# VectorE makes the lower parts of five weight units in the first FFN chunk, and the input forms are made in another order

## What is computed

```
def swiglu_ffn(h, w_gu, w_down):            # w_gu 1024 x 5632, w_down 2816 x 1024
    gate, up = jnp.split(h @ w_gu, 2, axis=-1)
    return (jax.nn.silu(gate) * up) @ w_down

for layer in range(2):
    x = x + mixer(rms_norm(x, mix_norm[layer]))
    x = x + swiglu_ffn(rms_norm(x, ffn_norm[layer]), w_gu[layer], w_down[layer])
```

## Time and profile before

| | before |
|---|---|
| median of 3 runs | 2703.15 us (2702.84 to 2703.3) |
| the profiled execution's own time | 2702.78 us |
| its span | 2701.0 us |
| TensorE busy in the span | 99% |
| VectorE, ScalarE, GpSimd busy | 47%, 31%, 47% |
| granted TensorE clock, mean | 0.998 |

### The profile page before, as it was taken

One profiled execution on the slowest core, in us unless ns is written; L12 is line 12 of the kernel. 1 busy time (PEld: TensorE's weight loads), 2 busy tenths in 40 slices (PEclk: granted clock), 3 DMA queues, 4 the chain that ended last, 5 costly groups with the idle time before them and its releaser, 6 DMA issues.

```text
span 2701.0 us, 35201 instructions
## 1 busy us (share of the span) xinstructions
PE 2672.0 (99%) x12017; PEld 2213.0 (82%) x12017; DVE 1273.9 (47%) x1719; ACT 831.3 (31%) x1388; POOL 1267.7 (47%) x1208
## 2 busy tenths in 40 slices
PE   8999999999999999999999999999999999999998
PEld 6888888888888788888888788888887888888887
DVE  8333322323334854444444447365688444444444
ACT  4120120120124533333333515234365222222224
POOL 4324323323423455655555454363454556655555
PEclk9999999999999999999999999999999999999999
DMA  4101102111111111111121021111111111111212
GB/s 143 44 28 63 44 28 63 47 32 59 48 36 44 51 51 54 47 47 54 53 64 51 27 60 44 36 55 40 44 55 47 55 54 47 47 47 55 69 50 83
DMA packets 173768, 139.29 MB, mean 52 GB/s; under 512 B 9200, under 2 KB 143472, under 8 KB 173680
## 3 DMA queue, kind: packets, MB, share of 16 engines
q1 hardware_dynamic: 171584, 133.46, 16.2%
q10 hardware_dynamic: 2096, 4.62, 0.5%
HBM read 132.81 MB, written 5.24 MB: 51 GB/s over the span
## 4 chain that ended last, share of the span: by engine, by line
PE 95%; DVE 3%; ACT 1%; issue 1%; DMA 0%; SPq 0%; DVEq 0%
PE ps L773 31%; PE ps L777 31%; PE ps L776 31%; DVE f_h_lo L2144 1%; PE ps L1085 0%; PE ps L1009 0%; PE ps L849 0%; PE ps L911 0%; DMA residual<-in_x 0%; DVE gate_buf L2082 0%; DVE f_h_lo L2133 0%; DVE h_sum_a L2133 0%; DVE gate_buf L2222 0%; ACT f_h_hi L1581 0%; DVE h_sum_a L2158 0%
## 5 line engine op out<-in xcount | busy, mean ns | idle before, releaser
L602 POOL TENSOR_TENSOR f_w_lo<-f_raw,f_w_hi 128x512 fp32r<-128x512 f32 x270 | 357.5, 1326 | 449.6 <-ACT f_w_hi L1532 364.6
L773 PE MATMUL ps<-f_h_hi,f_w_hi 128*128 128x512 f32 x1232 | 481.1, 390 | 3.6 <-DVE f_h_lo L2144 2.3
L777 PE MATMUL ps<-f_h_hi,f_w_lo 128*128 128x512 f32 x1232 | 479.5, 389 | 0.0
L776 PE MATMUL ps<-f_h_lo,f_w_hi 128*128 128x512 f32 x1232 | 479.4, 389 | 0.0
L560 POOL TENSOR_TENSOR small<-w_raw 128x1 f32<-128x1 f32 x200 | 59.5, 297 | 804.6 <-PE ps L773 794.1
L2333 DVE TENSOR_TENSOR residual<-ps,residual 128x512 f32<-128x512 f32 x352 | 239.4, 691 | 170.5 <-PE ps L777 170.4
L773 PEld LDWEIGHTS ps<-f_h_hi,f_w_hi 128*128 128x128 f32 x1232 | 231.2, 188 | 57.2 <-issue 4.4
L1532 ACT ACTIVATE f_w_hi<-f_raw 128x512 fp32r<-128x512 f32 x246 | 155.1, 631 | 382.9 <-PE ps L777 382.8
L777 PEld LDWEIGHTS ps<-f_h_hi,f_w_lo 128*128 128x128 f32 x1232 | 231.3, 188 | 48.3
L776 PEld LDWEIGHTS ps<-f_h_lo,f_w_hi 128*128 128x128 f32 x1232 | 231.3, 188 | 47.2
L773 PE MATMUL ps<-f_w_hi,f_act_hi 128*128 128x512 f32 x688 | 267.8, 389 | 0.0
(11 more groups left out here) (305 smaller groups left out, 4643.8 us busy)
## 6 DMA issues: line engine op xcount, KB each, us to landing
f_raw<-in_ffn_w_gu SPq DMA_DIRECT2D x176, 256.0 KB, 3.3
w_raw<-in_ret_w_in SPq DMA_DIRECT2D x96, 256.0 KB, 2.8
f_raw<-in_ffn_w_down SPq DMA_DIRECT2D x88, 256.0 KB, 2.8
w_raw<-in_lru_w_in SPq DMA_DIRECT2D x48, 256.0 KB, 2.9
w_raw<-in_ret_w_out SPq DMA_DIRECT2D x32, 256.0 KB, 2.6
w_raw<-in_lru_w_out SPq DMA_DIRECT2D x24, 256.0 KB, 2.6
residual<-in_x SPq DMA_DIRECT2D x8, 512.0 KB, 7.2
out_y<-residual SPq DMA_DIRECT2D x7, 512.0 KB, 2.6
```

What stands on the lines that cost most here:

```text
L602: nc.gpsimd.tensor_tensor(lo, src, hi.bitcast(F32), ALU.subtract).then_inc(f_wready, 1)
L773: m = nc.tensor.matmul(o, l_hi, r_hi, start=start, stop=False, skip_group_check=onto)
L776: nc.tensor.matmul(o, l_hi, r_lo, start=False, stop=False, skip_group_check=onto)
L777: return nc.tensor.matmul(o, l_lo, r_hi, start=False, stop=stop, skip_group_check=onto)
```

## The change

- VectorE makes the lower parts of units 4 to 8, that is (0,1), (1,1), (0,2), (1,2) and (0,3), by a new function `unit_lower`: one TENSOR_TENSOR of two SBUF operands each, with a wait for the units before and for ScalarE's upper part. GpSimd no longer makes these; it makes its last two sums `sum_4` on either side of unit 3's lower part and then waits until nine units are ready before it goes on with unit 9.
- VectorE's order in the stretch becomes: T1l 3, unit 4, T3 1, unit 5, T3 2, T3 3, T2 0, T3l 0, Q22l 0, unit 6, T3l 1, T2 1, T3l 2, T3l 3, Q22l 1, unit 7, T2 3, Q22l 3, unit 8, T2l 0, T2 2, T2l 1, T2l 2, T2l 3, Q22l 2, and then T4 as before.
- ScalarE's order becomes: T3h 0, 1, unit 6, T3h 2, 3, Q22h 0, unit 7, Q22h 1, Q22h 3, T2h 0, unit 8, T2h 1, T2h 3, Q22h 2, T2h 2, unit 9, and then as before.
- TensorE's program is the same but for the counts it waits for.

```diff
 HN_ACT = (...
-          + [("T3h", k) for k in FOUR] + [("Q22h", k) for k in (0, 1, 3, 2)] + [("T2h", k) for k in FOUR]
+          + [("T3h", k) for k in FOUR] + [("Q22h", 0), ("Q22h", 1), ("Q22h", 3), ("T2h", 0), ("T2h", 1), ("T2h", 3)]
+          + [("Q22h", 2), ("T2h", 2)]
 HN_DVE = (...
-          + [("T3", k) for k in (1, 2, 3)] + [("T2", k) for k in (0, 1, 3, 2)] + [("Q22l", 0)] + [("T3l", k) for k in FOUR]
-          + [("Q22l", 1), ("Q22l", 3)] + [("T2l", k) for k in FOUR] + [("Q22l", 2)]
+          + [("T3", k) for k in (1, 2, 3)] + [("T2", 0), ("T3l", 0), ("Q22l", 0), ("T3l", 1), ("T2", 1), ("T3l", 2)]
+          + [("T3l", 3), ("Q22l", 1), ("T2", 3), ("Q22l", 3), ("T2l", 0), ("T2", 2), ("T2l", 1), ("T2l", 2), ("T2l", 3)]
+          + [("Q22l", 2)]
 # GpSimd, first_units
+                sum_4(0)
                 lower(1, 4, raws[1][3])
-                sum_4(0)
-                lower(0, 1, f_in_sum(0))
-                lower(1, 1, f_in_sum(1))
                 sum_4(1)
-                lower(0, 2, raws[0][1])
-                lower(1, 2, raws[1][1])
-                summed(0, 3)
-                lower(0, 3, raws[0][0])
-                summed(1, 3)
+                pool.wait_ge(f_wready, units + AT_FIRST[1, 3])
                 lower(1, 3, raws[1][0])
 # ScalarE, norm_by_halves_act
                 unit(5)
-                for k in FOUR:
-                    from_sum(H_T3, k, t_b, "T3")
+                from_sum(H_T3, 0, t_b, "T3")
+                from_sum(H_T3, 1, t_b, "T3")
+                unit(6)
+                from_sum(H_T3, 2, t_b, "T3")
+                from_sum(H_T3, 3, t_b, "T3")
                 fourth(0)
-                unit(6)
+                unit(7)
                 fourth(1)
                 fourth(3)
+                from_sum(H_T2, 0, t_a, "T2")
+                unit(8)
+                from_sum(H_T2, 1, t_a, "T2")
+                from_sum(H_T2, 3, t_a, "T2")
                 fourth(2)
-                unit(7)
-                from_sum(H_T2, 0, t_a, "T2")
-                from_sum(H_T2, 1, t_a, "T2")
-                unit(8)
                 from_sum(H_T2, 2, t_a, "T2")
-                from_sum(H_T2, 3, t_a, "T2")
                 unit(9)
 # VectorE, norm_by_halves
+                def unit_lower(u, p):
+                    units, j = chunk_no(layer, 0) * F_UNITS, AT_FIRST[u, p]
+                    src = f_in_sum(u) if p == 1 else f_in_raw(4 * u + {2: 1, 3: 0}[p])
+                    hi, lo_ = f_unit(j)
+                    dve.wait_ge(f_wready, units + j)
+                    dve.wait_ge(f_whi, units + j + 1)
+                    TT(lo_, src, hi.bitcast(F32), ALU.subtract).then_inc(f_wready, 1)
 ...
                 lower(H_T1, 3, t_a, "T1h")
+                unit_lower(0, 1)
+                t_3(1)
+                unit_lower(1, 1)
+                t_3(2)
+                t_3(3)
+                t_2(0)
+                lower(H_T3, 0, t_b, "T3h")
+                plain(H_Q22, 0, 12, "Q22h")
+                unit_lower(0, 2)
+                lower(H_T3, 1, t_b, "T3h")
+                t_2(1)
+                lower(H_T3, 2, t_b, "T3h")
+                lower(H_T3, 3, t_b, "T3h")
+                plain(H_Q22, 1, 13, "Q22h")
+                unit_lower(1, 2)
+                t_2(3)
+                plain(H_Q22, 3, 15, "Q22h")
+                unit_lower(0, 3)
+                lower(H_T2, 0, t_a, "T2h")
+                t_2(2)
                 for k in (1, 2, 3):
-                    t_3(k)
-                for k in (0, 1, 3, 2):
-                    t_2(k)
-                plain(H_Q22, 0, 12, "Q22h")
-                for k in FOUR:
-                    lower(H_T3, k, t_b, "T3h")
-                plain(H_Q22, 1, 13, "Q22h")
-                plain(H_Q22, 3, 15, "Q22h")
-                for k in FOUR:
                     lower(H_T2, k, t_a, "T2h")
                 plain(H_Q22, 2, 14, "Q22h")
                 t_4(0)
```

## The result

| | before | changed |
|---|---|---|
| median, 13 runs each | 2703.31 us (2702.84 to 2704.1) | 2708.99 us (2708.51 to 2710.17) |
| ratio | | 1.0022, 95% interval 1.0013 to 1.003 |
| profiled execution: own time, span | 2702.78, 2701.0 us | 2708.51, 2706.7 us |

The changed kernel is 5.7 us slower; 2709.4 was forecast. Start with the page of the changed kernel, busy shares and then the chain of waits: TensorE's share of the chain falls from 95% to 93%.

A forecast was written before the change was run, and what follows sets the result against it. VectorE was taken to bound the stretch before product 11. Per layer, 4.18 us gained against 3.00 of added instructions, 2.44 of waits and new collisions gave 3.25 us late; twice that, 6.5, on 2702.78 led to 2709.4 us, range 2703.0 to 2711.5.

The forecast's parts named there:

- VectorE bounds the stretch: Product 4 to product 11: VectorE busy 22.14 of 22.58 us, so a delay of its T4 pieces arrives whole at product 11.
- Four lost turns against five instructions, 4.18 against 3.00: VectorE, T1l 3 to T4 0: four collisions with GpSimd vanish, gaining 4.18 us; five added lower parts cost 3.00 us.
- The waits on ScalarE, 2.44 us: VectorE waits on ScalarE ahead of Q22l 0, Q22l 3, unit 8 and T2l 2: 0.31, 0.91, 0.40 and 0.82 us.
- Who gets in at 906: GpSimd's unit 9 at 906.00 against VectorE's T2l 3 at 906.10: GpSimd goes first, costing T2l 3 1.10 us.
- the first rival: VectorE keeps its turn at 906, GpSimd starting after T2l 3: T4 3 2.65 us late, 2708.1 us in all; chance 0.24.
- The T4 stage of the rival: In the first rival, T4 0 waits 0.47 us; T4l 0 is held 0.27 by ScalarE's delay and 0.65 by collision.
- Unit 9 costed at nothing: GpSimd's later unit 9 costs nothing, GpSimd being idle and the unit needed only by product 9.
- `sum_4(0)` costed at nothing, in GpSimd's idleness: Moving this sum ahead of unit 3 costs nothing, falling into GpSimd's 34 us of idleness there.
- The sum: Both layers lose 3.25 us at product 11: 2 x 3.25 = 6.5 us on the profiled execution's 2702.78 us.

The follow-up runs named there:

- e3: Kernel before, with VectorE making the five lower parts but T2 0 to 3 kept together and ScalarE's list unchanged: 2704.47 us against 2703.59.
- e8: Changed kernel, same five units on VectorE, each T2 put well ahead of its Q22l and ScalarE's list following: 2704.48 us against 2703.39 before.
- e6: Changed kernel with GpSimd's lower parts of units 9 and 10 made for 1 of 512 columns: 2708.59 us, 1.0018 of before.
- e1: Kernel before with the whole change in layer 0's first FFN chunk only: 2705.81 us against 2703.59.
- e2: Kernel before with the whole change in layer 1's first FFN chunk only: 2706.48 us against 2703.59.
- e9: Kernel before with only GpSimd's sum_4(0) moved ahead of unit 3, in layer 1 behind a wait for Q11l 0: 2699.48 us against 2703.45.
- e5: Kernel before with only GpSimd's sum_4(0) moved ahead of unit 3's lower part, both layers: 2699.85 us against 2703.39.
- e11: As e10, but units 9 and 10 stay on GpSimd, so five units on VectorE: 2701.18 us against 2703.45 before.
- e10: Changed kernel in e8's order, units 9 and 10 also on VectorE, GpSimd's sums placed beside bank-reading work: 2700.55 us against 2703.45 before.

## Why the prediction was right, and where it was not

- *VectorE bounds the stretch.* Right: in the traces of all runs product 11 starts 3.44 to 3.47 us behind T4 3 (3.45 before, 3.45 in the changed kernel).
- *Four lost turns against five instructions, 4.18 against 3.00.* Right; e3 puts T4 0 at 904.92, the sum to 0.01 us.
- *The waits on ScalarE, 2.44 us.* Right: 2.28 measured from start to start (0.23, 0.85, 0.44, 0.76 for the forecast 0.31, 0.91, 0.40, 0.82); T4 0 at 907.24 for 907.36 before collisions. e8 takes the waits away and gets 2.24 us back.
- *Who gets in at 906.* Wrong: I chose GpSimd going first, 0.10 us ahead of T2l 3. It came at 905.99 as forecast (906.00), but VectorE's T2l 3 had started at 905.97 and not at 906.10, since the waits ahead of it were 0.16 us shorter, and GpSimd waited (1.82 us). That is the first rival, with its price nearly: 2.45 us measured a layer, 2.65 in the rival and 3.25 in my forecast. The difference of 0.1 us could not be had from the rows, and the range held both.
- *The T4 stage of the rival.* Nearly right as a sum: 1.31 us is lost between T4 0 and T4 3. T4l 0 starts 2.15 us behind T4 0 and not 1.45, that is 0.70 for the rival's 0.47 and 0.27, and then loses a turn of 0.62 (0.65 in the rival). By e6 only this second turn has a price of its own; the first would be lost to ScalarE's T4h 0 anyway.
- *Unit 9 costed at nothing.* Right, but not by its cover: GpSimd ends it at 907.81 and product 9 starts at 907.96, 0.3 us later than it would without a hole. This is hidden, since product 10 waits for VectorE anyway (911.35).
- *`sum_4(0)` costed at nothing, in GpSimd's idleness.* Wrong, twice. I looked at layer 0's row, where GpSimd had been idle for 34 us; in layer 1 it is only 23 us, and their beginning lies beside VectorE's scaling: 0.9 us (e1, e2, e9). And in the kernel before the same move is worth 2.1 us a layer (e5), of which the change uses half: with units 4 and 5 off GpSimd T1l 3 is free by that alone, and T1l 2 still loses its turn, to sum_4(1) behind unit 3 (1.68 us to the next start).
- *The sum.* 2.45 + 0.87 + 2.38 = 5.7 where I had 2 x 3.25 = 6.5. That the total came this close is in part luck: a turn too many in each layer (1.7 us) and a collision not seen (0.9 us) went opposite ways.

The Trainium skill (SBUF — State Buffer, section "Who interferes with whom") says that a VectorE instruction with at most one SBUF input, outside the modes that use both port pairs, does not contend with GpSimd, and one with two does where GpSimd's reads SBUF. The traces agree: 0.66 from start to start beside GpSimd for bank-reading ones in e5, 1.7 for those with two SBUF inputs. The scaling of e2 (TENSOR_SCALAR, one large SBUF input, 1.43 beside GpSimd) is a case in which one input did not keep it clear of GpSimd; that it ran in such a mode, no trace here shows.

What stays open: which of two waiting instructions of VectorE and GpSimd goes first. It was seen both ways, and no run here separates the causes. The traces of the two stretches do sort by time of arrival, where VectorE ran two-SBUF-input instructions of ordinary length (0.68) back to back. When GpSimd came 0.11 to 0.16 us ahead of VectorE's next such start, it went first (its rows are 1.34 to 1.39 us long). When it came 0.17 to 0.57 us ahead, it stood by until VectorE came to an instruction that reads a bank (2.40 to 2.88 us), as in e8:
```profile
903.17 2.40 POOL L612 TENSOR_TENSOR f_w_lo<-f_raw,f_w_hi 128x512 fp32r<-128x512 f32 x1 [14.33 <-ACT f_w_hi L1555]
```
Where VectorE's running instruction had itself just lost a turn, GpSimd went in at its end though it came 0.5 us ahead. This is read off the traces; no run varied the arrival alone.

## What to carry to other kernels

Where two engines take turns at a port, first ask which of their instructions meet: moving one GpSimd instruction of 1.3 us so that three fell beside PSUM-reading work won 2.1 us a layer, more than it won together with five or seven instructions moved to the other engine (1.0 in e11 and 1.3 in e10). A GpSimd instruction that is taken off one place also moves the ones behind it: look where they come to lie, as units 9 and 10 did in the T4 stage. A result that is needed right behind the step that sets it off on another engine costs the full round trip of some 1.5 us; put two or three instructions between. And a step that is moved "into idle time" has to be looked up in every place where the code runs, not in one.

## What the runs showed of the hardware

- A 128x512 TENSOR_SCALAR of VectorE with one SBUF operand of that size took about 0.4 us from start to start, and 1.43 us while GpSimd ran TENSOR_TENSOR instructions; one with a PSUM bank and one SBUF operand stayed at 0.66.
- GpSimd's lower part of 1 column instead of 512 still took 0.71 us when it came while VectorE ran one of its own with two SBUF inputs, and 0.19 when VectorE was idle.
- The round trip VectorE, ScalarE, VectorE took 1.45 to 1.51 us for 128x512, of which 0.6 to 0.7 is ScalarE's work.
